# The second mixer's softplus without the absolute value: a clamp on VectorE in front of the exponential

## The reference

```python
z = jnp.einsum('bthd,bshd->bhts', q[:, t0:t1], kb) * scale
before = s_idx < t_idx
log_beta = jax.nn.log_sigmoid(z)
log_1m_beta = jnp.where(before, jax.nn.log_sigmoid(-z), 0.0)
tail = lax.cumsum(log_1m_beta, axis=3, reverse=True) - log_1m_beta
a = jnp.where(before, jnp.exp(log_beta + tail), 0.0)
outs.append(jnp.einsum('bhts,bshd->bthd', a.astype(vb.dtype), vb))
```

## Time and profile before

| | |
|---|---|
| median of 3 runs | 2124.94 us (2124.16 to 2127.75) |
| the profiled execution | 2125.2 us, of it span 2123.1 us |
| TensorE busy | 2070.0 us, 97% of the span |
| VectorE busy | 1088.1 us, 51% |
| ScalarE busy | 753.4 us, 35% |
| the mixer's rounds | about 904 to 988 us |

### The profile page before, as it was taken

The page is one execution under the profiler, slowest core; times in us unless marked ns, Lnnn a source line. Parts: engine busy times, 40 slices in busy tenths (PEclk is TensorE's granted clock), DMA queues, the critical chain, the costliest instruction groups (busy, mean ns, idle before and its releaser), DMA issues.

```text
span 2123.1 us, 28504 instructions
## 1 busy us (share of the span) xinstructions
PE 2070.0 (97%) x11649; PEld 1714.7 (81%) x11649; DVE 1088.1 (51%) x1397; ACT 753.4 (35%) x1040; POOL 219.9 (10%) x196
## 2 busy tenths in 40 slices
PE   7999999999999999989999999999999999999998
PEld 7887788888888888866888888888787878888886
DVE  4764665554454453354554354456676435354453
ACT  6444432532222341475522222231574243222221
POOL 3000220400000040000400000141302010000001
PEclk9999999999999999999999999999999999999999
DMA  6231001222222322101132222334222212222221
GB/s 248 79 115 45 21 22 39 82 100 99 99 86 92 119 80 99 41 21 73 67 111 88 99 99 99 119 114 138 96 80 80 100 40 96 98 89 93 99 99 60
DMA packets 28336, 186.99 MB, mean 88 GB/s; under 512 B 3536, under 2 KB 3664, under 8 KB 6480
## 3 DMA queue, kind: packets, MB, share of 16 engines
q1 hardware_dynamic: 25200, 173.48, 22.8%
q0 software_dynamic: 2320, 11.01, 1.5%
q10 hardware_dynamic: 720, 1.11, 0.1%
HBM read 181.39 MB, written 2.10 MB: 86 GB/s over the span
## 4 chain that ended last, share of the span: by engine, by line
PE 91%; DVE 5%; ACT 3%; DMA 1%; issue 1%; ACTq 0%; DVEq 0%
PE PS L571 89%; ACT Y L1473 1%; DVE Y L2187 1%; DVE WL L2190 1%; ACT WH L1473 1%; DVE Y L2190 1%; DVE SQ L2190 0%; DMA STG<-weights 0%; DMA MX<-mem_t 0%; PE PS L789 0%; PE PS L598 0%; ACT ABUF L1473 0%; ACT SQ L1473 0%; DVE QKV L2190 0%; DVE HL L2190 0%
## 5 line engine op out<-in xcount | busy, mean ns | idle before, releaser
L571 PE MATMUL PS<-HH,WH 128*128 128x512 f32 x1544 | 608.4, 394 | 6.3 <-DVE HL L2190 4.1
L571 PE MATMUL PS<-HH,WL 128*128 128x512 f32 x1544 | 601.9, 390 | 0.0
L571 PE MATMUL PS<-HL,WH 128*128 128x512 f32 x1544 | 591.5, 390 | 0.0
L2190 DVE TENSOR_TENSOR WL<-STG,WH 128x2048 fp32r<-128x2048 f32 (+1 forms) x159 | 358.6, 2255 | 264.5 <-ACT WH L1473 264.4
L1473 ACT ACTIVATE WH<-STG 128x2048 fp32r<-128x2048 f32 (+2 forms) x167 | 307.2, 1839 | 522.6 <-PE PS L571 520.6
L571 PEld LDWEIGHTS PS<-HH,WH 128*128 128x128 f32 x1544 | 290.3, 188 | 71.6 <-DVE HL L2190 5.8
L571 PEld LDWEIGHTS PS<-HH,WL 128*128 128x128 f32 x1544 | 290.4, 188 | 60.4
L571 PEld LDWEIGHTS PS<-HL,WH 128*128 128x128 f32 x1544 | 290.5, 188 | 59.6 <-issue 0.7
L571 PE MATMUL PS<-UPH,WH 128*128 128x512 f32 x832 | 324.3, 390 | 1.4 <-DVE UPL L2187 1.4
L571 PE MATMUL PS<-UPH,WL 128*128 128x512 f32 x832 | 323.9, 389 | 0.0
L571 PE MATMUL PS<-UPL,WH 128*128 128x512 f32 x832 | 323.8, 389 | 0.0
(11 more groups left out here) (319 smaller groups left out, 2087.8 us busy)
## 6 DMA issues: line engine op xcount, KB each, us to landing
STG<-weights SPq DMA_DIRECT2D x159, 1024.0 KB, 4.8
KEY_STG<-weights POOLq DMA_DIRECT2D x4, 1024.0 KB, 6.1
XT<-x_t SPq DMA_DIRECT2D x2, 1024.0 KB, 9.1
KEY_X<-mem_t POOLq DMA_DIRECT2D x2, 1024.0 KB, 6.3
out_t<-Y SPq DMA_DIRECT2D x8, 256.0 KB, 2.0
STG<-weights SPq DMA_DIRECT2D x4, 256.0 KB, 5.4
MX<-mem_t ACTq DMA_DIRECT2D x4, 256.0 KB, 7.6
CON<-consts SPq DMA_DIRECT2D x1, 1024.0 KB, 8.9
```

The costliest lines, as they stand in the source:

```text
L571: return pe.matmul(o, l, r, start=start, stop=stop, **kw)
L2190: return dve.tensor_tensor(o, a, b, op)
```

## The change

The absolute value is taken out. VectorE writes the smaller of score and 40 into SP (`stick_clamp`, semaphore sb_cl in place of sb_az), ScalarE takes exp of that without a scale and log of one plus that, and VectorE takes the larger of score and logarithm. Up to 40 this is log(1 + exp(z)), and above 40 it is z itself.

```diff
@@ ScalarE
-            def stick_size(n):
-                e = n % 2
-                act.wait_ge(sems["sb_z"], n + 1)
-                if n >= 2:
-                    act.wait_ge(sems["sb_rc"], n - 1)
-                A(SP[e], PSF[:, SB_BASE[e]:SB_BASE[e] + SB_ALL], ACT.Abs).then_inc(sems["sb_az"], 1)
             def stick_exp(n):
-                act.wait_ge(sems["sb_az"], n + 1)
-                A(SP[n % 2], SP[n % 2], ACT.Exp, scale=-1.0).then_inc(sems["sb_e"], 1)
+                act.wait_ge(sems["sb_cl"], n + 1)
+                A(SP[n % 2], SP[n % 2], ACT.Exp).then_inc(sems["sb_e"], 1)
...
             def stick_breaking():
-                stick_size(1)
                 stick_exp(1)
...
                     if n + 2 < 12:
-                        stick_size(n + 2)
                         stick_exp(n + 2)
...
                 elif i == 5:
                     value_tiles(1, 1)
-                    stick_size(0)
@@ VectorE
+            def stick_clamp(n):
+                e = n % 2
+                dve.wait_ge(sems["sb_z"], n + 1)
+                if n >= 2:
+                    dve.wait_ge(sems["sb_rc"], n - 1)
+                dve.tensor_scalar(SP[e], PSF[:, SB_BASE[e]:SB_BASE[e] + SB_ALL], 40.0, None, ALU.min).then_inc(sems["sb_cl"], 1)
...
-                    stt(SP[e], PSF[:, SB_BASE[e]:SB_BASE[e] + SB_ALL], 0.0, SP[e], ALU.max, ALU.add).then_inc(sems["sb_sp"], 1)
+                    tt(SP[e], PSF[:, SB_BASE[e]:SB_BASE[e] + SB_ALL], SP[e], ALU.max).then_inc(sems["sb_sp"], 1)
...
+                stick_clamp(1)
                 softplus(0)
                 split_lo(R0["B.out"])
                 softplus(1)
                 for n in range(12):
                     e, g = n % 2, n // 2
+                    if n + 2 < 12:
+                        stick_clamp(n + 2)
                     dve.wait_ge(sems["sb_a"], n + 1)
...
                 memory_half(1, i)
+                if i == 5:
+                    stick_clamp(0)
```

More of the change, by code:

```diff
@@ L111 @@
 out_ready ow par_in gains_in pool_mm pool_s pool_z qd rcnt_in rk rope_cos rope_done rope_in
-df_b rows_in rows_tr rq rs rsc rv sb_a sb_az sb_cap sb_e sb_l sb_m sb_o sb_rc sb_sp sb_half sb_t sb_u sb_z
+df_b rows_in rows_tr rq rs rsc rv sb_a sb_cl sb_cap sb_e sb_l sb_m sb_o sb_rc sb_sp sb_half sb_t sb_u sb_z
 sc_act sc_dve sc_k sc_ws spread sig silu sq sqa sqrt ss st tile t1 u_mm u_sb uh ul vn vr_mm xf zeroed vrow vtr w_sb
```

## The result

| | changed kernel | kernel before |
|---|---|---|
| median | 2134.35 us, 5 runs (2132.93 to 2136.15) | 2124.94 us, 5 runs (2123.22 to 2127.75) |
| ratio | 1.0044, 95% interval 1.0029 to 1.0058 | |
| profiled execution | 2134.3 us, span 2132.2 | 2125.2 us, span 2123.1 |

The change costs 9.4 us where 7.3 were forecast; the time lies in the stated range, near its upper end. A second series of the changed kernel, of ten executions, gave 1.0045 (1.0030 to 1.0060); its median, 2136.13 us, lies 0.9 above that range, beside a kernel before that was 0.2 us slower than here. The forecast's terms are called the start (from scores(1) to the exponential of round 2), the pairs (two rounds each, up to the exponential of round 10) and the end (from there to the exponential of round 11).

What follows compares the result with a forecast made beforehand. The second mixer was taken as bound by the even rounds' loop through ScalarE, TensorE and VectorE, 13.65 us. Terms 3.5 + 1.7 + 1.6 + 0.5 = +7.3 us gave a median of 2132.2, range 2127.0 to 2135.2.

Steps and rivals of the forecast that it cites:

- the start: Scores(1) to round 2's exponential: clamp(1) queued ahead of softplus(0) delays tails(0); +3.5 us.
- the pairs: Four pairs of rounds, exponential(2) to exponential(10): 14.05 us each instead of 13.64; +1.6 us.
- the end: Round 11's exponential behind round 10's: softplus(11) and tails(11) fall behind a later log(11), 6.55 against 6.08; +0.5 us.
- a second loop through VectorE: Steady rounds: odd clamp waits for even softplus, even exponential for odd log; about 14.05 us, longer than the first loop's 13.90.
- The clamp's price: Each VectorE clamp, 128x1280 from PSUM: 1.50 us, bounds 0.98 and 1.79, against 1.25 for the activation replaced.
- Rival (a): Clamp in all rounds is quick, 0.98 us: +3.0 in all, 2127.9 us; chance 10%.
- the old dip: Low clock before the change in tails(1), 5.42 us at mean granted clock 0.69; its cost counted as already in 924.46.
- The low clock: At tails(0), after TensorE idles 4.6 us: same loss as tails(1) had, 5.42 - 3.74 = +1.7 us.
- Rival (c): Clamp of 1.79 us, +3.0, 2135.2; or low clock reaching tails(1) or scores(2), 2133 to 2134; chance 15%.
- (b): No low clock at tails(0) after the idle 4.6 us: +5.6, 2130.5 us; chance 13%.
- (d): Steady rounds: ScalarE's relief outweighs VectorE's load; at TensorE's own 12.9 four pairs would give -3.0; chance 2%.
- (e): All twelve activations replaced but mixer loops left alone, another wait covering clamp and start: within 0.2%; chance 2%.

Runs made afterwards that it cites:

- the odd and even runs: Clamp only in odd rounds from 3 (ratio 1.0001), or only in even rounds from 2 (0.9998), other rounds by the old form; ratios to the kernel before.
- the filled kernel: Changed kernel plus discarded TensorE matmuls, five between scores(1) and tails(0), three ahead of tails(11): 2130.48 us, 1.0028 to the kernel before.

## Why the prediction was right, and where it was off

**Direction and mechanism.** Slower, by the start and by a second loop through VectorE: right. The start was undone by moving one line, and the loop shows itself in the odd and even runs by its length and by what the exponential waits for. One slip in the working does no harm: 947.97 + 3.74 - 938.08 is 13.63, and 13.65 includes the hand-over to the next exponential.

**The clamp's price**, 1.50 us taken between 0.98 and 1.79: right (1486 ns). The two sections of the Trainium skill's "VectorE: DVE Perf Modes" both allow this: "The perf-mode tier table" gives an upper limit of twice the base rate, and the estimated 0.83 took the limit for the rate; "Why PSUM operands drop a tier" allows 32-bit data the base rate alone, and 1486 ns beside the two-input operation's 1490 agrees. Rival (a) is out.

**The start, +3.5 without the clock**: right. 26.90 less tails(0)'s excess of 3.03 is 3.52 over before; 25.26 less 1.40 is 3.51; and the filled kernel, without any low clock, 3.52. The figure is measured, as it was forecast, against the one trace of before, whose tails(1) were slowed ("the old dip's cost is already in 924.46"). Against the starts without that dip, 19.56 and 19.37, the filled kernel's 23.87 is 4.3 to 4.5 us longer. How often executions of the kernel before have the dip is not shown; that the traced one has it is chance, which the forecast took over with its rows.

**The low clock, +1.7**: the term that was mis-sized. That it would come was right. In three traces with this pause tails(0) lost 3.0, 1.4 and 1.65 us, 2.0 on average against 1.7, but the first trace shows what the step left out: the clock fell early in the pause and stayed low for all but the last half microsecond of tails(0), while before, tails(1) was only partly in it. And a second place was missed, the pause ahead of tails(11), first before, then now:

```profile
981.34 0.49 PE L571 MATMUL PS<-TAIL,CON 128*128 128x128 f32 x2 [1.11 <-DVE TAIL L2190]
986.47 0.49 PE L571 MATMUL PS<-TAIL,CON 128*128 128x128 f32 x2 [1.84 <-DVE TAIL L2179]
```

Behind it tails(11) were slowed by 1.7 us in the first trace and in the kernel with clamp(1) moved, but not in the second trace, with the absolute value at the start or with clamps in odd rounds, all with the same 1.84. Rival (c) had a low clock that reaches on, to tails(1) or scores(2), which no trace shows; the second stretch lies elsewhere. The three other terms measured 3.52 + 1.88 + 0.54 = 5.9, so of the measured 9.4 some 3.5 us are left for the clock, against the 1.7 forecast. This is a remainder, not a measurement: it takes in low clock in stages that the change leaves alone. Filling both pauses took away 3.6 by the ratio, which fits, with intervals too wide to settle it more closely.

**The pairs, +1.6**: 14.11 measured against 14.05 reckoned, +1.9. Right, and with it that cap(n) behind the clamp costs nothing.

**The end, +0.5**: right where the clock is full (6.62 against 6.08).

**The other rivals.** (b), no low clock, occurred in no trace of the changed kernel; made by force it gave 1.0028, +5.9 (+5.3 by the medians) with the added work, where +5.6 was said. (d) does not happen with the clamp on VectorE; with both it and the absolute value gone the pairs do fall to TensorE's own pace, 12.74, a little under the 12.9 of the sum of its parts, since the rows of its groups overlap at their edges (scores(5) end at 930.39 and tails(4) start at 930.31, for one). (e) is out.

## What to carry to other kernels

An operation moved to a less busy engine takes its place in that engine's order, and everything behind its wait is moved too: here twelve moved operations of nearly equal length cost 9 us on an engine that is half idle, and one line's place decided over half of it, part of it through the clock. Follow the loop that sets the pace, and then look for the second longest, which passes through the engine that got the work. Before an operation is moved, see whether another one that reads the same data can do it on the way; here that gave 5 to 6 us.

## What the runs showed that I had not expected

The clock outlasts the pause. In the first trace of the changed kernel TensorE was idle from 898.9 to 900.28, ran scores(1) for 1.39 us, and the granted clock fell soon after 902, half a microsecond into the long pause; it stayed at the half level through the pause and for most of tails(0), to about 912.5, although TensorE worked from 906.30 on (windows, as above):

```profile
900.00:902.00 2.00, 1.39 (x20) 1.19 (x20) 0.29 (x1) 2.00 (x2) 0.00 (x0) 1.00 0.00 0
902.00:904.00 2.00, 0.00 (x0) 0.00 (x0) 2.00 (x2) 0.79 (x2) 0.00 (x0) 0.56 0.00 0
...
911.00:913.00 2.00, 2.00 (x4) 0.62 (x3) 0.03 (x1) 0.00 (x0) 0.00 (x0) 0.63 0.88 373
```

And where it falls differs from one execution to the next in code that is the same: the first mixer lost over 3 us at 333 and 363 us in one trace and nothing in another. Of the ten traces six have both of these stretches at the half level and four have neither, although TensorE's pause ahead of the second, at about 361 to 365 us, is 2.65 or 2.66 us long in all ten. Ten executions of the changed kernel in one series lay between 2128.64 and 2140.74 us, six of the kernel with clamps in rounds 0 and 1 between 2128.51 and 2133.11. So the length of a pause does not by itself decide: 2.65 us there, 1.71 ahead of scores(2) and 1.84 ahead of tails(11) were followed by a low clock in some traces and not in others, and what decides stays open. Only the pause of 4.6 us was followed by it in every trace that left it empty.
